# Two deferred tiles turned behind the first part of the next product

## The chip, the cores and the metric

The kernel runs on one core of a Trainium2 chip. The metric is the device time of one execution in microseconds; the median of the runs counts.

## The reference, cut to what matters

The program computes two blocks of two layers each on 512 tokens of width 1024. The first block mixes an mLSTM, a Fourier mix and a convolution, each layer followed by an MLP. The second block, where the change acts, projects the normed tokens by a wide matrix `w_in_2` and feeds a retention, a sparse attention with an index (`dsa`) and a gated linear attention (`gla`). At the start of each of its layers stand the projections of the index:

```python
h = rms_norm(x, pre_norm[l]) * (1.0 + scale[:, None]) + shift[:, None]
p = split_proj(h @ w_in[l])
q_idx = rope(q_idx, pos, IDX_ROT, ROPE_THETA)                        # 4 heads of 64: tiles DIQ 0, DIQ 1
k_idx_f = rope(k_idx[:, :, None], pos, IDX_ROT, ROPE_THETA)[:, :, 0] # 64 wide, laid twice: tile DIK
```

`rope` is x * cos + (x with its halves exchanged and one negated) * sin. The vectors `shift`, `scale` and `gate` come from products of a conditioning vector with `ada_w`, which the kernel spreads over its run.

## The kernel before, in words

**One list of steps for all engines.** `Order` writes a list of steps, and each of the five engine programs walks through it and emits its own share of a step (`mm` a part of a product, `ev` its evacuation from PSUM, `post` a piece of work after the evacuation, `split` the preparation of weights). The order of the list is so the order of each engine's instructions; a step that an engine has no share in doesn't touch its queue. Between engines there are semaphores. There is no second queue: an instruction that waits holds up all behind it on its engine.

**Products.** A float32 product of a weight tile (128 columns, 8 slices of 128 rows) and 512 tokens is 24 matmuls of 128x512: for each slice k, weight high half by token high half, weight low by token high, weight high by token low (L1012 to L1014). The weights come from HBM in slabs through a ring of six slots by SP (L920); ACT makes the high half (`split`, L2162, into WHI, two buffers), POOL the low half (L2572, in place in the ring as RGR). The split of unit u waits for the last matmul of unit u - 2. `place` puts the `split` steps into the list by an estimate of the time, in which `post` and `ev` cost nothing.

**Parts.** `task` cuts a product of 512 tokens into three parts: slices 0 to 2 (nine matmuls), 3 to 5 (nine), 6 and 7 (six). `run` puts the parts into the list. Behind each part comes what is woven in from beside (`weave`) and, behind the first, the turning of a modulation tile made by `filling` (`early`, list `soon`). Behind the last part it puts the `post` steps of the tiles that were left in `after`, and then the product's own `ev`. A tile whose evacuation is followed by more TensorE work (`roped`, `few`, `vheads`, the last tiles of a norm's output, `gateY`) is put into `after` by `task`, so each is worked on behind the next product, when its evacuation is over.

**abreast.** The first two products behind a norm are made side by side, slice by slice, since their tokens' slices come one by one (L356 to L379). Here `after` takes several: at the start of a layer of the second block the tiles DIQ 0 and DIQ 1, and with them the modulation tile (`ada`) that `self.laid` holds ready.

**The post of a rotated tile.** ACT evacuates the product into a buffer RAWS (L2322). TensorE multiplies it by a 128x128 permutation into bank PB7 (L1176, plain float32, two records), after DVE has read what PB7 held before. DVE multiplies the raw tile by the cosines (L1529), waits for TensorE, multiplies PB7 by the sines (L1532) and adds (L1534).

**The post of a modulation tile.** ACT copies the product's rows to WT (L2228), TensorE turns them by four small matmuls (L1142, L1143) into the bank of the tile, DVE adds the bias and writes MOD (L1515). The bank is free for the next product only then.

**The place.** In each of the two layers: DIQ 0 and DIQ 1 abreast (banks 1 and 0), `ada` (bank 1), DIK (bank 0), `post` DIQ 0, `post` DIQ 1, `post` ada, then `few` (20 columns wide, bank 1), `post` DIK, `post` few (transposes at L1185), and the product RQ 0.

Of the kernel before, what the change touches and what calls it, by code (L numbers as in the profile page):

```python
# [143 lines left out]
class Order:  # L144
# [54 lines left out]
    def run(self, n, parts, us):  # L199

        for part in parts:
            self.step("mm", n, part)
            self.early()
            self.weave(us / len(parts))
        for m in self.after:
            self.step("post", m)
        self.after = []
        self.step("ev", n)
        self.filling(us)
# [2511 lines left out]
```

## Time and profile before

| | |
|---|---|
| median of 3 runs | 3375.01 us (3374.52 to 3376.37) |
| the profiled execution | 3374.18 us |
| its span | 3372.4 us |
| mean granted TensorE clock | 0.939 |
| TensorE (PE) busy | 3063.9 us, 91% |
| DVE, ACT, POOL busy | 1419.1, 1010.1, 1044.4 us |
| PE idle before L1176, in all | 7.7 us behind DVE's L1534, four records |

How to read it: PE is the matmul side of TensorE, PEld its weight loads, DVE, ACT and POOL are VectorE, ScalarE and GpSimd, SP issues the loads. Times in the timelines are us from the start of the span. "idle before <-releaser" is the time that the engine stood still before the instruction, and the instruction that ended it. The granted clock is 1.00 at 2.4 GHz and 0.50 at 1.2 GHz.

### The profile page before, as it was taken

The numbers are of one execution on the slowest core, as the hardware profiler recorded it, in microseconds if no ns is written. First come the engines' busy times: TensorE is split into PE (matmuls) and PEld (weight loads), VectorE is DVE, ScalarE is ACT, GpSimd is POOL, SyncE is SP. The second block draws the span as 40 slices with busy tenths as digits, with TensorE's granted clock in tenths as the row PEclk, the third lists the DMA queues.
The fourth block names the chain that finished last, engine by engine and source line by source line (L and its number), as shares of the span: only waits on it lengthen the run. The fifth ranks groups of instructions, "written<-read, shape, count | busy, mean of one in ns | idle before, by whom it ended". The sixth has DMA issues, their size and how long they took to land.

```text
span 3372.4 us, 41180 instructions
## 1 busy us (share of the span) xinstructions
PE 3063.9 (91%) x16748; PEld 2460.5 (73%) x16748; DVE 1419.1 (42%) x2601; ACT 1010.1 (30%) x1640; POOL 1044.4 (31%) x508
## 2 busy tenths in 40 slices
PE   6899779899999979968999989999889989998898
PEld 4688568788888857757777776776668766775686
DVE  4583442513324356243521134734472346444722
ACT  3213432312213231342332332233423322334232
POOL 1121114122222312114344433232336422322455
PEclk9999878999999889978999989999999899999999
DMA  5332341111111123411322221121112221111122
GB/s 200 122 111 102 124 155 57 58 63 64 63 64 63 50 82 119 144 63 63 104 94 94 93 77 63 63 69 63 56 44 88 70 75 64 68 63 57 51 75 69
DMA packets 77707, 275.37 MB, mean 82 GB/s; under 512 B 8512, under 2 KB 10304, under 8 KB 77392
## 3 DMA queue, kind: packets, MB, share of 16 engines
q1 hardware_dynamic: 75824, 268.91, 23.7%
q10 hardware_dynamic: 1696, 3.84, 0.3%
q8 instruction: 133, 2.18, 0.3%
q14 instruction: 54, 0.44, 0.0%
HBM read 270.62 MB, written 2.10 MB: 81 GB/s over the span
## 4 chain that ended last, share of the span: by engine, by line
PE 78%; DVE 12%; ACT 4%; issue 3%; POOL 1%; DMA 1%; SPq 0%; DVEq 0%; ACTq 0%; POOLq 0%
PE pb L1012 19%; PE pb L1014 18%; PE pb L1013 18%; PE pb L1122 2%; PE pb L1034 2%; PE pb L1036 2%; PE pb L1035 2%; PE pb L961 2%; PE pb L1052 1%; PE pb L1054 1%; PE pb L1053 1%; DMA RG<-in_W_dram 1%; PE pb L1080 1%; DVE AR L1674 1%; POOL RGR L2572 1%
## 5 line engine op out<-in xcount | busy, mean ns | idle before, releaser
L2572 POOL TENSOR_TENSOR RGR<-RG,WHI 128x1024 fp32r<-128x1024 f32 x354 | 862.5, 2437 | 1896.1 <-ACT WHI L2162 1896.1
L2162 ACT ACTIVATE WHI<-RG 128x1024 fp32r<-128x1024 f32 x354 | 370.7, 1047 | 414.1 <-PE pb L1014 288.6
L1012 PE MATMUL pb<-HI,WHI 128*128 128x512 f32 (+1 forms) x880 | 379.0, 431 | 21.6 <-DVE MOD L1515 6.5
L1013 PE MATMUL pb<-HI,RGR 128*128 128x512 f32 (+1 forms) x880 | 355.2, 404 | 0.0
L1014 PE MATMUL pb<-LO,WHI 128*128 128x512 f32 (+1 forms) x880 | 355.2, 404 | 0.0
L1012 PE MATMUL pb<-HR,WHI 128*128 128x512 f32 (+1 forms) x768 | 278.8, 363 | 16.7 <-POOL RGR L2572 10.1
L1014 PE MATMUL pb<-HR,WHI 128*128 128x512 f32 (+1 forms) x768 | 277.8, 362 | 0.0
L1013 PE MATMUL pb<-HR,RGR 128*128 128x512 f32 (+1 forms) x768 | 277.5, 361 | 0.0
L1012 PE MATMUL pb<-HIDR,WHI 128*128 128x512 f32 (+1 forms) x768 | 273.7, 356 | 1.1 <-ACT RLT L2308 0.8
L1014 PE MATMUL pb<-HIDR,WHI 128*128 128x512 f32 (+1 forms) x768 | 274.7, 358 | 0.0
L1013 PE MATMUL pb<-HIDR,RGR 128*128 128x512 f32 (+1 forms) x768 | 274.2, 357 | 0.0
L1012 PEld LDWEIGHTS pb<-HI,WHI 128*128 128x128 f32 (+1 forms) x880 | 169.3, 192 | 92.5 <-issue 42.1
L1707 DVE TENSOR_TENSOR RLT<-RLT 128x256 f32<-128x256 f32 (+1 forms) x96 | 117.3, 1222 | 206.7 <-ACT RLT L2308 206.4
L1014 PEld LDWEIGHTS pb<-LO,WHI 128*128 128x128 f32 (+1 forms) x880 | 168.5, 191 | 44.7 <-issue 1.6
L1012 PE MATMUL pb<-HH,WHI 128*128 128x512 f32 (+1 forms) x464 | 173.9, 375 | 29.7 <-POOL RGR L2572 18.9
L1013 PEld LDWEIGHTS pb<-HI,RGR 128*128 128x128 f32 (+1 forms) x880 | 169.3, 192 | 38.9 <-issue 5.4
L1012 PEld LDWEIGHTS pb<-HR,WHI 128*128 128x128 f32 x768 | 146.9, 191 | 47.3 <-issue 24.3
L1013 PE MATMUL pb<-HH,RGR 128*128 128x512 f32 (+1 forms) x464 | 166.8, 359 | 0.0
L1014 PE MATMUL pb<-HL,WHI 128*128 128x512 f32 (+1 forms) x464 | 166.6, 359 | 0.0
L1014 PEld LDWEIGHTS pb<-HR,WHI 128*128 128x128 f32 x768 | 147.0, 191 | 22.9
L1012 PEld LDWEIGHTS pb<-HIDR,WHI 128*128 128x128 f32 x768 | 144.2, 188 | 26.5 <-issue 2.3
L1013 PEld LDWEIGHTS pb<-HR,RGR 128*128 128x128 f32 x768 | 147.1, 192 | 22.5
(407 smaller groups left out, 5637.4 us busy)
## 6 DMA issues: line engine op xcount, KB each, us to landing
RG<-in_W_dram SPq DMA_DIRECT2D x504, 512.0 KB, 3.5
XCX<-in_xT_dram ACTq DMA_DIRECT2D x4, 512.0 KB, 12.1
out_dram<-XCX SPq DMA_DIRECT2D x8, 256.0 KB, 2.1
CS<-in_CST_dram ACTq DMA_DIRECT2D x1, 1027.0 KB, 4.8
XCC<-in_ctxT_dram SPq DMA_DIRECT2D x4, 256.0 KB, 13.9
CS<-in_CST_dram SPq DMA_DIRECT2D x1, 523.0 KB, 4.7
RG<-in_W_dram SPq DMA_DIRECT2D x2, 256.0 KB, 2.7
RG<-in_W_dram SPq DMA_DIRECT2D x2, 128.0 KB, 3.5
```

The source lines that it names most:

```text
L961: i = e.matmul(PB[p["banks"][0]][32 * g:32 * g + 32, 0:256], CV[:, :, 4 * h + g], wt[:, g, :], start=h == 0, stop=h == 1, tile_position=(0 ...
L1012: e.matmul(out, hi[:, k, :], xh, start=k == order[0], stop=False)
L1013: e.matmul(out, lo[:, k, :], xh, start=False, stop=False)
L1014: i = e.matmul(out, hi[:, k, :], xl, start=False, stop=k == order[7])
L1034: e.matmul(out, xh[:, sl], hi[:, k, :], start=h == 0 and i0 % per == 0 and k == 0, stop=False)
L1035: e.matmul(out, xh[:, sl], lo[:, k, :], start=False, stop=False)
L1036: i = e.matmul(out, xl[:, sl], hi[:, k, :], start=False, stop=p["final"] and ends and k == nk - 1)
L1052: e.matmul(out, hi[:, k, :], xh, start=k == 0, stop=False)
L1122: m = e.matmul(sum_at(tag, c), squares_at(tag, i)[:, a:a + 128], ones[:, 0:1], start=k == 0 and c == first, stop=k == 7 and c == 5)
L1707: e.tensor_tensor(r, r, r, MUL).then_inc(*up("evacV", ("hidden", i)))
L2162: e.activation(WHI[:, u % 2, 0:n], RG[:, s % RING, 0:n], ACT.Copy).then_inc(*up("weightsA", u))
L2572: e.tensor_tensor(RGR[:, s % RING, 0:n], RG[:, s % RING, 0:n], WHI[:, u % 2, 0:n].bitcast(F32), SUB).then_inc(*up("weightsG", u))
```

## The change

`run` gets two lines. Behind the first part of a product (and behind each further one, where something is still left) it now puts the `post` steps of all tiles in `after` but the last. The last keeps its place behind the whole product.

```diff
@@ -201,6 +201,8 @@
         for part in parts:
             self.step("mm", n, part)
             self.early()
+            while len(self.after) > 1:
+                self.step("post", self.after.pop(0))
             self.weave(us / len(parts))
         for m in self.after:
             self.step("post", m)
```

## Rows read from the trace of the kernel before

**Rows 1.** The page: busy times, the chain by engine, the weight loads

```profile
PE 3063.9 (91%) x16748; PEld 2460.5 (73%) x16748; DVE 1419.1 (42%) x2601; ACT 1010.1 (30%) x1640; POOL 1044.4 (31%) x508
...
PE 78%; DVE 12%; ACT 4%; issue 3%; POOL 1%; DMA 1%; SPq 0%; DVEq 0%; ACTq 0%; POOLq 0%
...
RG<-in_W_dram SPq DMA_DIRECT2D x504, 512.0 KB, 3.5
```

**Rows 2.** Waits of TensorE, whole span: us in total, times, longest

```profile
PE pb L1012 <- DVE MOD L1515: 7.0, 4, 3.3
...
PE pb L1176 <- DVE AR L1534: 3.0, 2, 1.5
PE pb L1185 <- DVE AR L1534: 3.0, 2, 1.5
```

**Rows 3.** Timeline of the first place: start, us, engine, line, idle before

```profile
2019.95 0.47 PE L1012 MATMUL pb<-HI,WHI 128*128 128x512 f32 x1 [2.15 <-POOL RGR L2572]
...
2022.54 0.63 PE L1014 MATMUL pb<-LO,WHI 128*128 128x512 f32 x1
...
2022.96 0.63 PE L1012 MATMUL pb<-HI,WHI 128*128 128x512 f32 x1
...
2027.16 1.02 PE L1176 MATMUL pb<-AR,CS 128*128 128x512 f32 x2
2028.22 0.69 DVE L1532 TENSOR_TENSOR AR<-pb,TAB 128x512 f32<-128x512 f32 x1 [10.61 <-PE pb L1176]
2028.94 0.69 DVE L1534 TENSOR_TENSOR AR<-AR 128x512 f32<-128x512 f32 x1
...
2029.69 1.13 PE L1176 MATMUL pb<-AR,CS 128*128 128x512 f32 x2 [1.51 <-DVE AR L1534]
...
2030.65 0.28 PE L1142 MATMUL pb<-CS,WT 128*128 128x1 f32 x2
...
2030.79 0.36 PE L1143 MATMUL pb<-CS,WT 128*128 128x1 f32 x2
...
2031.41 2.34 POOL L2572 TENSOR_TENSOR RGR<-RG,WHI 128x1024 fp32r<-128x1024 f32 x1 [11.12 <-ACT WHI L2162]
2031.58 2.72 DVE L1534 TENSOR_TENSOR AR<-AR 128x512 f32<-128x512 f32 x1
2034.22 0.15 DVE L1515 TENSOR_TENSOR MOD<-pb,VC 128x2 f32<-128x2 f32 x1
...
2034.42 0.62 PE L1012 MATMUL pb<-HI,WHI 128*20 128x512 f32 x1 [3.27 <-DVE MOD L1515]
...
2038.22 0.40 PE L1012 MATMUL pb<-HI,WHI 128*20 128x512 f32 x1
...
2041.69 1.02 PE L1176 MATMUL pb<-AR,CS 128*128 128x512 f32 x2
```

**Rows 4.** Windows: stretch, length, PE PEld DVE ACT POOL busy, PEclk, DMA, GB/s

```profile
2021.00:2024.20 3.20, 3.20 (x9) 2.48 (x8) 0.00 (x0) 0.00 (x0) 0.00 (x0) 0.51 0.63 248
...
2034.50:2037.90 3.40, 3.40 (x9) 1.22 (x10) 0.47 (x1) 0.00 (x0) 0.00 (x0) 0.50 0.00 0
...
2042.80:2044.20 1.40, 0.00 (x0) 0.00 (x0) 1.33 (x2) 0.62 (x1) 0.64 (x1) 1.00 0.93 295
2044.90:2048.20 3.30, 3.30 (x9) 2.59 (x8) 0.00 (x0) 0.00 (x0) 1.49 (x1) 0.51 0.00 0
```

**Rows 5.** Timeline of the second place

```profile
2719.30 1.12 PE L1176 MATMUL pb<-AR,CS 128*128 128x512 f32 x2 [1.51 <-DVE AR L1534]
...
2724.03 0.62 PE L1012 MATMUL pb<-HI,WHI 128*20 128x512 f32 x1 [3.27 <-DVE MOD L1515]
```

**Rows 6.** Timeline around the first place: ada's turning, ACT, POOL, DVE

```profile
2016.27 0.28 PE L1142 MATMUL pb<-CS,WT 128*128 128x1 f32 x2
...
2016.80 0.16 DVE L1515 TENSOR_TENSOR MOD<-pb,VC 128x2 f32<-128x2 f32 x1 [4.44 <-PE pb L1143]
2016.91 0.69 DVE L1529 TENSOR_TENSOR AR<-AR,TAB 128x512 f32<-128x512 f32 x1
2017.21 0.59 ACT L2322 ACTIVATE AR<-pb 128x512 f32<-128x512 f32 x1
2017.45 2.84 POOL L2572 TENSOR_TENSOR RGR<-RG,WHI 128x1024 fp32r<-128x1024 f32 x2 [28.18 <-ACT WHI L2162]
...
2042.75 0.69 DVE L1532 TENSOR_TENSOR AR<-pb,TAB 128x512 f32<-128x512 f32 x1 [7.78 <-PE pb L1176]
```

## The prediction

> **What bounds the kernel.** The page comes first: TensorE is busy for 91% of the span, and 78% of the chain that ended last lies on it [rows 1]. A change therefore counts by what it does to the time in which TensorE stands still and to the clock at which it runs. Next, TensorE's waits [rows 2]. They are many and short. Three kinds lie where this change acts: 1.5 us before the rotation at L1176, 1.5 us before the transposes at L1185 (both twice), and up to 3.3 us before a product's first matmul at L1012, behind a DVE addition at L1515. Third, the order of the steps: `after` holds more than one entry at the start of `run` at only two places of the program, the first ordinary product (DIK) of each layer of the second block. There it holds three, the rotations of DIQ 0 and DIQ 1 and the turning of a modulation tile (ada), all left by `abreast`. Everywhere else, the norms' sums among them, at most one waits and the new loop doesn't turn. The timeline of the first place [rows 3] and windows over it [rows 4] carry the sum; [rows 5] show that the second repeats it to some hundredths of a us.
>
> **The place before** [rows 3]. DIK starts at 2019.95. Its 24 matmuls end where rotation 0 starts, at 2027.16: 7.21 us. Rotation 0 takes 1.02 us; then TensorE waits 1.51 us while DVE multiplies (0.69) and adds (0.69). Rotation 1 starts at 2029.69, the ada turning at 2030.65, and its small matmuls end at 2031.15. The next product (few) takes the bank in which the ada result sits. DVE empties that bank only behind rotation 1, and the addition L1534 there takes 2.72 us instead of 0.69, as it meets POOL's weight split (2031.41, 2.34 us). So L1515 runs at 2034.22 and few at 2034.42, after 3.27 us idle. Its 24 matmuls last until 2041.69, 7.27 us. From DIK's start to few's end: 21.74 us.
>
> **What the change does to each queue.** DVE, ACT, POOL and SP have no step between DIK's parts here, so their instructions keep their order. Only TensorE's changes: two rotations (four matmul records) move ahead of DIK's last 15 matmuls, the ada turning stays behind DIK, nothing is added. Queued behind the moved waits is the rest of DIK, so the 1.51 us for rotation 0 are still paid, now inside it. What goes is the wait for DVE's work on rotation 1, which gets the 15 matmuls as cover. The inputs are there in time: ACT has copied both by 2017.80, DVE has done its first multiplication by 2017.60 [rows 6].
>
> **The sum for the first place.**
> - DIK's first nine matmuls: 2019.95 to 2022.96 as before, 3.01 us.
> - Rotation 0 starts at 2022.96, with a granted clock of 0.5 (1.2 GHz) until 2024.2 or so [rows 4]. No row here shows a rotation begun at that clock. Its bounds are 1.02 us and twice that; the matmuls beside it take 0.42 us from start to start instead of 0.23, so I take 1.75. With 1.44 for DVE and 0.05 to resume it is 3.24, and rotation 1 starts at 2026.20. DVE meets no split here: POOL is through at 2020.29 and its next one needs ACT, behind DIK [rows 3, 6].
> - Rotation 1: about 0.86 to the next issue.
> - DIK's last 15 matmuls. The prices are those of few: nine in 3.80 us, 0.422 each, at the low clock, then 15 in 3.47, 0.231 each, at 2.4 GHz [rows 3, 4]. Does the clock hold? After the idle time before few, and after the 1.5 us behind few, the granted clock was 0.5 from 2034.5 to 2037.9 and from 2044.9 to 2048.2 [rows 4]. The moved stall is as long, so I take it that eight matmuls run slow here: 3.38 + 1.62 = 5.00 us. Bounds: none slow 3.5, all slow 6.3.
> - From DIK's end to few: the held ada tile was turned and added without a queue in front, from 2016.27 to 2016.96 [rows 6]; with 0.05 to resume 0.75 us, where there were 0.50 and 3.27. DVE's work on rotation 1 is done by 2028.6; a whole POOL split on top, 2.34, would still be covered.
> - few: 4.8 us of idle in two stalls stood before it and nine of its matmuls were slow. Now some 0.25 us stands there, and the low stretch is spent in DIK: 24 x 0.231 = 5.54. Bounds 5.5 and 7.3.
>
> Together 3.01 + 3.24 + 0.86 + 5.00 + 0.75 + 5.54 = 18.40 us against 21.74: **3.34 us less**. 3.0 of it is idle time; the rest is the clock.
>
> What is late next: DIK ends at 2032.1 instead of 2027.2. POOL's split for the product after few moves with it, from 2031.41 to about 2033.8, ends by 2036.2 and is wanted at 2041.2; 5 us of cover, beyond which each us would cost one. SP's load into DIK's slot goes out 4.9 us later and serves the fifth product after few, at least five times 5.5 us away; it lands in 3.5 us [rows 1].
>
> **Does it last?** DVE stood idle for 10.6 us before this place and for 7.8 us behind few [rows 3, 6], so no backlog reaches across, and the loads follow the matmuls. All that comes after moves up as a whole, and the second place saves as much: 6.7 us. The profiled execution took 3374.18 us, its span 3372.4; the median of the runs, 3375.01, is 0.83 above it. 3374.18 - 6.7 = 3367.5 for such an execution, **3368.3 us** for the median, 0.20% less. A measurement of this kernel tells about 0.2%, 6.75 us, from no change.
>
> **Rivals.**
> *The clock holds* inside DIK. Its rest then takes 3.5 us: 4.8 per place, 9.7 in all, 3365.3; if the fall behind few goes as well, 1.6 more per place, 3362. For it: the idle has matmuls close on both sides. Against it: a stall of that length (2042.8 to 2044.2) was followed by the low clock [rows 4]. The Trainium skill, on the page "TensorE: Matmul & The Clock Gate", section on HAM oscillation, puts the return to half rate down to long waits between groups of matmuls; by that rule this rival would be the outcome, and this trace, with its 1.5 us, disagrees.
> *Given back.* The idle goes, yet few runs nine matmuls slow beside DIK's eight. Then 3.34 - 9 x 0.19 = 1.6 per place: 3371.8. For it: each stall had a low stretch of its own. Against it: only 0.25 us is left before few.
> *Slower.* The stop inside DIK lets the clock fall and keeps it down through DIK's rest and few. Then 3.0 + 3.2 + 1.7 + 6.3 + 1.0 + 10.1 and 0.9 for the next rotation make 26.2 us, 4.5 lost per place: 3384. It decides from 24 slow matmuls behind rotation 0 on (the nine of before, and the 3.0 us of idle over 0.19 each). Against it: both times the clock came back after eight or nine matmuls without a break.
> *It doesn't do what it says*, as nowhere else do two entries wait. That is taken in above; if the two places didn't bring their 3.0 us either, the time would stay at 3375.
>
> **How the numbers follow.** Forecast 0.50, clock holds 0.28, given back or next to nothing 0.17, slower 0.05. The forecast's own spread, 3366.5 to 3370, lies across the bound of 0.2% at 3368.3, half on each side. Faster: 0.28 + 0.25 = 0.53. Same: 0.25 + 0.17 = 0.42. Slower: 0.05. The range runs from 3362.5 (both gains of the clock) to 3372.0 (given back).
>
> **What would show it.** Right: L1176 starts near 2023.0 and 2026.2, behind nine matmuls of DIK; no addition L1534 here takes over 0.7 us; few waits some 0.25 us, starts near 2032.8 and runs at the high clock; the granted clock is 0.5 in DIK's rest; the same about 686 us later; the span is near 3365.7. Wrong: over 1 us of wait before few, a low clock in few, a DVE operation of over 2 us at this place, or a new wait for POOL at the product behind few.

## The result, and the profile after

The changed kernel took **3358.3 us** (median of 4 runs, 3354.24 to 3359.23), the kernel before, run beside it, 3374.77 (4 runs, 3372.47 to 3376.37). The ratio is **0.9949**, its 95% interval 0.9932 to 0.9967: 16.5 us less, where 6.7 were forecast, and below the range that was given. Two further comparisons on other chips gave 0.9968 (0.9956 to 0.9979) and 0.9971 (0.9960 to 0.9983). The changed kernel is faster each time, by 0.3 to 0.5%. Its profiled run took 3354.24 us, its span 3352.1. Line numbers below are those of the kernel before plus 2.

The page after, its line of busy times, which answers to the first of [rows 1]:

```profile
PE 3055.5 (91%) x16748; PEld 2453.9 (73%) x16748; DVE 1416.1 (42%) x2601; ACT 1010.4 (30%) x1640; POOL 1044.4 (31%) x508
```

The same instructions. TensorE is busy for 8.4 us less (3063.9 to 3055.5) with the same 16748 matmuls, so a good part of the gain is matmuls that took less time, at a higher granted clock as the windows below show; DVE's 3.0 us less are about what it saves at the two places (7.80 to 5.96 us in each, by the windows further down), where it no longer meets POOL.

TensorE's waits, whole span (us in total, times, longest); they answer to [rows 2]:

```profile
PE pb L1178 <- DVE AR L1536: 3.0, 2, 1.5
PE pb L1187 <- DVE AR L1536: 3.0, 2, 1.5
PE pb L1014 <- DVE MOD L1517: 1.0, 4, 0.3
```

The two waits of 3.27 us are 0.25 now; the other two kinds stand as before. That is the 3.0 us per place of the forecast.

Timeline of the first place after; it answers to [rows 3]:

```profile
2019.95 0.47 PE L1014 MATMUL pb<-HI,WHI 128*128 128x512 f32 x1 [2.15 <-POOL RGR L2574]
...
2023.01 1.75 PE L1178 MATMUL pb<-AR,CS 128*128 128x512 f32 x2
...
2026.26 1.12 PE L1178 MATMUL pb<-AR,CS 128*128 128x512 f32 x2 [1.51 <-DVE AR L1536]
2026.82 0.80 PE L1014 MATMUL pb<-HI,WHI 128*128 128x512 f32 x1
...
2028.15 0.69 DVE L1536 TENSOR_TENSOR AR<-AR 128x512 f32<-128x512 f32 x1
...
2030.72 0.28 PE L1144 MATMUL pb<-CS,WT 128*128 128x1 f32 x2
...
2031.47 0.41 PE L1014 MATMUL pb<-HI,WHI 128*20 128x512 f32 x1 [0.25 <-DVE MOD L1517]
...
2032.61 2.40 POOL L2574 TENSOR_TENSOR RGR<-RG,WHI 128x1024 fp32r<-128x1024 f32 x1 [12.32 <-ACT WHI L2164]
...
2037.03 1.02 PE L1178 MATMUL pb<-AR,CS 128*128 128x512 f32 x2
```

The order is the one foreseen. POOL's split now starts at 2032.61, behind DVE's work on both rotations; the addition takes 0.69 us, where it took 2.72. The clock is another matter (windows of the changed kernel, columns as in [rows 4]):

```profile
2023.00:2026.20 3.20, 1.75 (x3) 0.33 (x1) 1.38 (x3) 0.00 (x0) 0.00 (x0) 0.77 0.04 14
2026.40:2030.60 4.20, 4.20 (x17) 3.08 (x18) 1.79 (x3) 0.00 (x0) 0.00 (x0) 1.00 0.02 4
...
2039.20:2042.50 3.30, 2.95 (x15) 2.47 (x16) 0.30 (x1) 0.18 (x1) 2.54 (x1) 1.00 0.18 71
```

The first stretch holds the stall inside DIK, the second the rest of DIK, at 1.00 where 0.5 was forecast. The third follows the 1.51 us stall behind few; before, the granted clock was 0.5 there [rows 4].

To compare whole traces I cut the program at four matmuls: a **place** runs from DIK's first matmul to the matmul 88 later, in RQ 1; a **remainder** from there to the next place or the last matmul. The windows of place 1, remainder 1, place 2, remainder 2, before:

```profile
2019.95:2052.63 32.68, 26.39 (x88) 16.28 (x89) 7.80 (x10) 3.65 (x6) 5.50 (x3) 0.79 0.19 66
2052.63:2709.55 656.92, 604.84 (x3187) 470.33 (x3186) 308.21 (x558) 208.91 (x327) 248.38 (x118) 0.96 0.21 66
2709.55:2742.17 32.62, 26.33 (x89) 16.17 (x89) 7.80 (x10) 3.65 (x6) 5.50 (x3) 0.79 0.18 66
2742.17:3359.02 616.85, 572.73 (x3030) 443.33 (x3029) 284.93 (x525) 193.04 (x302) 237.36 (x111) 0.98 0.19 63
```

and after:

```profile
2019.95:2046.42 26.47, 23.20 (x88) 14.24 (x89) 5.96 (x10) 3.65 (x6) 5.59 (x3) 0.94 0.23 79
2046.42:2699.29 652.87, 602.56 (x3188) 467.74 (x3186) 308.18 (x558) 208.92 (x327) 248.48 (x118) 0.96 0.21 67
2699.29:2725.75 26.46, 23.19 (x88) 14.34 (x89) 5.96 (x10) 3.65 (x6) 5.58 (x3) 0.94 0.23 78
2725.75:3338.65 612.90, 570.61 (x3031) 440.76 (x3029) 284.90 (x525) 193.06 (x302) 237.47 (x111) 0.98 0.19 63
```

Each place is 6.2 us shorter, not 3.3. And each remainder, in which the change moves no instruction, is 4.0 us shorter: 2.3 and 2.1 us of that are less time busy, 1.8 in each are less time standing still. 2 x 6.2 + 2 x 4.0 = 20.4 us; the rest of the program took as long in these two profiled runs (both reach the place at 2019.95), whose times are 3374.18 - 3354.24 = 19.9 us apart.

A window's mean clock gives the time at 1.2 GHz in it: (1 - PEclk) x 2 x length. Before, a place had 0.42 x 32.68 = 13.7 us at 1.2 GHz, the 3.27 us of idle before few among them, so 10.5 us of matmuls. After it has 0.12 x 26.47 = 3.2 us. Three stretches of matmuls ran at half rate before (at DIK's start, in few, behind few [rows 4]); one such stretch is left. The matmul time saved in a place, 26.39 - 23.20 = 3.2 us, is what this difference in the clock gave back.

### The profile page after: what moved, and what is told of

Its sections match the earlier page's. It is cut to its first block, busy times and chain, and to the rows that moved or that the text cites. A ratio compares the mean times of both kernels' runs of the same rounds, so it can differ in the third digit from the quotient of the medians.

```text
span 3352.1 us, 41180 instructions
## 1 busy us (share of the span) xinstructions
PE 3055.5 (91%) x16748; PEld 2453.9 (73%) x16748; DVE 1416.1 (42%) x2601; ACT 1010.4 (30%) x1640; POOL 1044.4 (31%) x508
## 4 chain that ended last, share of the span: by engine, by line
PE 78%; DVE 12%; ACT 4%; issue 3%; POOL 1%; DMA 1%; SPq 0%; DVEq 0%; ACTq 0%; POOLq 0%
PE pb L1014 19%; PE pb L1016 18%; PE pb L1015 18%; PE pb L1124 2%; PE pb L1036 2%; PE pb L963 2%; PE pb L1038 2%; PE pb L1037 2%; DMA RG<-in_W_dram 1%; PE pb L1054 1%; POOL RGR L2574 1%; PE pb L1056 1%; PE pb L1055 1%; PE pb L1082 1%; DVE AR L2085 1%
## 6 DMA issues: line engine op xcount, KB each, us to landing
XCC<-in_ctxT_dram SPq DMA_DIRECT2D x4, 256.0 KB, 13.9
```

## The experiments

Three theories were to be told apart. **Idle and clock**: the removed wait gives its own 3.0 us, and the low stretches behind it go too. **Collision**: what mattered was DVE's addition beside POOL's split. **Alignment**: the remainders turn on how TensorE stands to the changes of its clock when it comes out of a place. Beside every group of kernels the kernel before ran on the same chip: 3373.55 us (30 runs) beside the first four, 3375.51 (15) beside e5 to e8, 3370.61 (16) beside e9 to e11. The lengths here are of the profiled run of each, read as above; the medians are of all runs. The expectations cut at other matmuls: their places are about 2 us shorter than those of the table (24.5 for 26.47), their remainders about 1 and 2 us longer (657.9 for 656.92, 619.0 for 616.85).

| kernel | median us | ratio (95%) | place 1 | remainder 1 | place 2 | remainder 2 |
|---|---|---|---|---|---|---|
| before | 3374.77 | | 32.68 | 656.92 | 32.62 | 616.85 |
| e8_before | 3376.82 (1 run) | | 32.67 | 656.93 | 32.64 | 616.79 |
| after | 3358.30 | 0.9949 | 26.47 | 652.87 | 26.46 | 612.90 |
| e1_again | 3361.47 | 0.9968 (0.9956-0.9979) | 26.43 | 656.96 | 26.45 | 612.81 |
| e10_change | 3362.27 | 0.9971 (0.9960-0.9983) | 26.45 | 656.89 | 26.48 | 612.83 |
| e2_fill | 3372.37 | 0.9994 (0.9986-1.0003) | 29.52 | 657.05 | 29.52 | 619.93 |
| e3_pool_later | 3364.81 | 0.9973 (0.9964-0.9981) | 25.86 | 654.18 | 31.51 | 614.46 |
| e4_layer0 | 3371.67 | 0.9996 (0.9988-1.0005) | 26.40 | 656.90 | 32.66 | 616.92 |
| e5_shift | 3372.66 | 0.9992 (0.9983-1.0001) | 33.35 | 652.82 | 33.32 | 612.85 |
| e6_spread | 3363.27 | 0.9964 (0.9950-0.9977) | 25.93 | 656.81 | 25.92 | 616.79 |
| e7_spread_few | 3357.56 | 0.9947 (0.9935-0.9960) | 22.77 | 659.22 | 21.16 | 615.44 |
| e9_ada_first | 3366.65 | 0.9988 (0.9979-0.9997) | 26.09 | 659.89 | 26.10 | 616.77 |
| e11_spread_few | 3357.17 | 0.9959 (0.9947-0.9972) | 21.17 | 655.37 | 22.80 | 619.80 |

**e1_again: the change once more.** No edit.

> The changed kernel once more, to see how far its time and its places of low clock are the same from run to run. Two theories for the 10 us beyond the forecast. Clock theory: with the stall before few gone, TensorE's granted clock stays at 1.0 in few and in the product behind it, at both places, in every run: 16 us less, ratio 0.9950 to 0.9956, and the two places take 24.5 us each from DIK's start as in the first trace. Chance theory: which stretches get the low clock is luck, the place's true gain is 3.3 us each and the first runs were lucky: ratio nearer 0.998, and the low stretch shows up inside DIK's rest or behind few in this trace.

3361.47 us. Its trace repeats both places to 0.04 us and remainder 2 to 0.1, while remainder 1 has the length of before. The third trace of the change, e10_change, was taken beside e9 and e11:

> The changed kernel, beside the spread version on one chip. Places of 24.5 and 24.3 us, the second layer's end in its short form, 615.0; the first layer's remainder 653.8 or 657.9 by where the first 2020 us leave the clock. Median 11 to 16 us below the kernel before.

3362.27 us, with the same four lengths as e1. So 6.2 us per place and 4.0 in remainder 2 repeat; the 4.0 in remainder 1 came in one of three traces. By the four lengths e1 and e10 are 16.4 us below the kernel before, by medians 12.1 and 8.3, which is less than e10's expectation (11 to 16). In the traces a part of such a difference lies in front: the same code up to the first place took between 2019.06 and 2027.90 us, so the times of two traced runs carry some us of that, and the cut lengths don't. Whether it explains the medians too, no run shows: they hold runs without a trace, and of the kernel before only two runs were cut up.

In e1 the low stretch of place 1 isn't at DIK's start (window 2023.14:2026.40) but behind few (2042.80:2046.10). Windows of e1_again, columns as before:

```profile
2023.14:2026.40 3.26, 3.19 (x11) 1.96 (x11) 0.03 (x1) 0.00 (x0) 0.34 (x1) 1.00 0.76 292
2029.60:2033.80 4.20, 3.95 (x21) 2.91 (x20) 1.52 (x4) 1.30 (x2) 0.00 (x0) 1.00 0.06 17
2042.80:2046.10 3.30, 3.30 (x10) 2.60 (x10) 0.00 (x0) 0.00 (x0) 0.55 (x1) 0.61 0.00 0
```

Its place 2 has it at DIK's start again. The length of the place is the same either way, but the remainder behind it isn't. The change was traced in seven places, two in each of its three traces and one in that of e4_layer0 below. In four the low stretch lay at DIK's start, and the remainder behind was the short one; in three it lay behind few (place 1 of e1, of e10 and of e4), and the remainder was the long one. For e10, at DIK's start and behind few:

```profile
2020.30:2026.00 5.70, 4.19 (x14) 2.48 (x15) 1.99 (x3) 0.00 (x0) 0.29 (x1) 1.00 0.47 184
2039.10:2042.50 3.40, 3.40 (x10) 2.63 (x9) 0.00 (x0) 0.00 (x0) 1.35 (x1) 0.50 0.00 0
```

So in these seven places the clock at DIK's start already told which remainder would follow. That is an order seen in the traces; no run set it on purpose.

**e2_fill: the waits stay, TensorE works in them.** Five throwaway matmuls behind rotation 0, twelve behind the ada turning, into a bank that is free there; nothing uses their result.

```diff
-        for m in self.after:
+        queued = len(self.after)
+        for i, m in enumerate(self.after):
             self.step("post", m)
+            if queued == 3 and i == 0:
+                self.step("spin", 5, 3)
+        if queued == 3:
+            self.step("spin", 12, 3)
...
+        def spin(count, bank):
+            for _ in range(count):
+                e.matmul(PB[bank][:, :], HI2[:, 0, 0:128], HI2[:, 1, :], start=True, stop=True)
```

> The kernel before, with throwaway matmuls (5 and 12 of 128x512 into a free bank, 1.2 and 2.8 us) put into the two stalls of each place. The waits stay as they are, TensorE is only busy in them. Clock theory: few's nine slow matmuls become fast (1.75 us per place) and the product behind few too, perhaps; with what follows in the layer 3 to 5 us per place, so 3367 or less, ratio 0.996 to 0.998. Idle theory (only the time in which TensorE stands still counts): no gain, ratio 1.000. Chance theory: ratio between 0.999 and 1.001.

Timeline and window of e2_fill, place 1:

```profile
2030.62 1.12 PE L1181 MATMUL pb<-AR,CS 128*128 128x512 f32 x2 [0.36 <-DVE AR L1543]
...
2031.94 2.97 PE L1487 MATMUL pb<-HI 128*128 128x512 f32 x12
2035.42 0.41 PE L1017 MATMUL pb<-HI,WHI 128*20 128x512 f32 x1 [0.51 <-DVE MOD L1524]
```
```profile
2022.41:2051.93 29.52, 27.14 (x105) 17.67 (x106) 7.87 (x10) 3.64 (x6) 5.57 (x3) 0.94 0.20 73
```

The waits for DVE are all still there, and only 0.36 and 0.51 us of the two stalls are left unfilled. The work added brings nothing, and yet the place is 3.16 us shorter: its mean clock is 0.94 in place of 0.79, with the same 3 us or so at 1.2 GHz as under the change. That is the clock's share of the 6.2 us by itself: with the two stalls filled, two of the three slow stretches are gone. In the sum half of the 2 x 3.1 us was lost, since remainder 2 came out 3.1 us longer, and the median shows nothing (0.9994), where 0.996 to 0.998 was expected.

**e3_pool_later: the collision alone.** The kernel before, but POOL's split of RQ 0's weights waits until DVE has done with rotation 1.

```diff
+        held_back = {}
+        for m, p in enumerate(o.pieces):
+            if p["how"] == "few":
+                held_back[p["unit"] + 1] = m - 3
...
+            if u in held_back:
+                e.wait_ge(*at("evacV", ("roped", held_back[u])))
```

> The kernel before, but at the two places POOL's weight split for the product behind few waits until DVE's addition for rotation 1 is through. If the 2.72 us addition is DVE held up by POOL, it takes 0.69 us, few starts 2.03 us earlier and waits 1.24 instead of 3.27 us: 4.1 us less in all, ratio 0.9988, and more only if the clock changes with it. If the addition is long for another reason, it stays at 2.7 us and the ratio at 1.000 or above. The clock theory adds: two stalls of 1.5 and 1.2 us are still there, so few still starts at the low clock.

Timeline and windows (places 1 and 2) of e3_pool_later:

```profile
2037.99 0.69 DVE L1534 TENSOR_TENSOR AR<-AR 128x512 f32<-128x512 f32 x1
...
2038.81 0.41 PE L1012 MATMUL pb<-HI,WHI 128*20 128x512 f32 x1 [1.24 <-DVE MOD L1515]
...
2038.85 2.75 POOL L2579 TENSOR_TENSOR RGR<-RG,WHI 128x1024 fp32r<-128x1024 f32 x1 [10.62 <-DVE MOD L1515]
```
```profile
2027.90:2053.76 25.86, 21.60 (x89) 13.49 (x89) 5.77 (x10) 3.64 (x6) 5.92 (x3) 1.00 0.23 79
2707.94:2739.45 31.51, 27.25 (x89) 16.44 (x90) 5.77 (x10) 3.64 (x6) 5.90 (x3) 0.78 0.18 66
```

The addition takes 0.69 us, few waits 1.24 instead of 3.27. So 2.03 of the 3.27 us were the collision, and with the split out of the way 8.7 us of the program went (0.9973) with no matmul moved, more than the 2 x 2.03 us of idle time and the 0.9988 expected from them. The two places have the same instructions, the same idle time (4.26 us) and lengths 5.65 us apart: one had the full clock throughout, the other 0.44 x 31.51 = 13.9 us at 1.2 GHz. This is what the clock alone can do to such a place. It also limits what e2 says: in place 1 here the two stalls ahead of few (1.51 and 1.24 us) cost no low stretch at all.

**e4_layer0: half the change.** The new loop in the first of the two layers only.

```diff
+            while len(self.after) > 1 and self.pieces[n]["l"] == 0:
+                self.step("post", self.after.pop(0))
```

> The change in the first layer of the second block alone. Clock theory and idle theory both: half of the whole gain. If the gain is made in each layer by itself, 8 us less, ratio 0.9976, with 6.2 us of it at the place and the rest in the remainder of that layer. If the second layer gains only because the first shifts its phase against the clock's, the second place here is not as before, and the ratio is away from 0.9976 by more than 0.001.

Place 1 has the new length (26.40), place 2 the old one (32.66), and remainder 2, whose code and place are those of before, has the old length to 0.07 us. The expected ratio, 0.9976, wasn't reached: remainder 1 took its long form. The median moved by 1.9 us only, with an interval that holds no change, where the four lengths give 6.2. The profiled run reached the first place 3.6 us later than that of before; whether the other runs did so too, no trace tells.

**e5_shift: added work.** The kernel before, with three throwaway matmuls ahead of RQ 1 in each layer; the waits of the place are untouched.

```diff
+        if self.pieces[n]["how"] == "roped" and self.pieces[n]["dst"] == "RQ" and self.pieces[n]["jj"] == 1:
+            self.step("spin", 3, 3)
```

> The kernel before, with three throwaway matmuls (0.7 us) in front of the product RQ 1 in each layer of the second block, behind the place, and nothing else. Phase theory: the remainder of a layer has a long and a short form (657.9 or 653.8 us in the first layer, 619.0 or 615.0 in the second, the same to 0.1 us in all traces so far), and which it takes hangs on how TensorE stands to the clock's changes when it leaves the place. The 0.7 us put the second layer into the short form: its end takes 615.7 us with the added work instead of 619.0, and the first layer 654.5 or stays at 658.6. So 2.5 to 6.6 us less in spite of added work. Theory of work alone: 1.4 us more, both remainders 0.7 longer, no low stretch fewer.

Windows of e5_shift: remainder 1, remainder 2:

```profile
2054.56:2707.38 652.82, 602.57 (x3188) 468.32 (x3186) 307.47 (x558) 208.29 (x327) 248.40 (x118) 0.96 0.21 67
...
2740.70:3353.55 612.85, 570.63 (x3030) 441.32 (x3029) 284.22 (x525) 192.43 (x302) 237.39 (x111) 0.98 0.20 63
```

Each place is 0.7 us longer, as the three matmuls cost, and each remainder 4.0 us shorter, to 0.05 us the two remainders of `after`. So a remainder can be short with every wait of the place left standing and no engine relieved. That the 0.7 us are the cause is likely for remainder 2, which was long in both traces of the kernel before; it rests on this one trace, and it doesn't tell coming later from TensorE being busier just ahead. It isn't steady: the eleven runs lie between 3367.55 and 3379.95 us, and the median (0.9992) can't be told from no change.

**e6_spread: all three pieces spread over DIK.** The ada turning and rotation 0 behind its first part, rotation 1 behind its second.

```diff
-        for part in parts:
+        if len(self.after) == 3:
+            early, self.after = [self.after[2:] + self.after[:1], self.after[1:2], []], []
+        else:
+            early = [[]] * len(parts)
+        for i, part in enumerate(parts):
...
+            for m in early[i]:
+                self.step("post", m)
```

> From the kernel before: behind DIK's first part the ada turning and rotation 0, behind its second part rotation 1, nothing behind the whole. The 1.5 us stall inside DIK goes, since the second part covers DVE's work on rotation 0, and the 0.25 us before few. Both theories: 1.7 us of idle less per place than in the changed kernel, so a place of 22.8 us instead of 24.5 and 30.7, about 3.5 us below the changed kernel, ratio 0.995 to 0.996. Clock theory: no low stretch within the place but the one at DIK's start or the one behind few. If the stall was needed for nothing but DVE, this is the better version.

Place 1 of e6_spread:

```profile
2024.35:2050.28 25.93, 24.42 (x89) 15.79 (x89) 6.60 (x11) 3.65 (x6) 5.57 (x3) 0.87 0.23 81
```

TensorE stands still for 25.93 - 24.42 = 1.51 us, where 3.27 are left under the change: 1.76 us less idle. Yet the place is only 0.54 us shorter, because 0.26 x 25.93 = 6.7 us of it are at 1.2 GHz instead of 3.2, and remainder 2 is the long one (616.79). 3363.27 us, 12.2 below the kernel before, where the change gave 16.5, 12.1 and 8.3: no better than the change, and short of its expected ratio.

**e7_spread_few and e11_spread_few: no wait left.** e6, and few's transposes go behind the first part of RQ 0.

```diff
+        if tasks[-1]["how"] == "few":
+            self.soon, self.after = self.soon + self.after, []
+            return
```

> As the run before, and the transposes of few go behind the first part of RQ 0, so the 1.5 us stall behind few goes too. Place of 21.3 us, another 1.5 us less idle per place, and the low stretch behind few can't start: 1.6 us more where it was there. 3358 us or less, ratio 0.9945 to 0.9955. If the remainder of a layer falls into its long form by the new phase, 4 us per layer are given back, to 3363.

> The spread version with the transposes of few behind RQ 0's first part, again, for a comparison with the change on one chip. Places of 19 to 21 us against 24.4: 9 us less by the places, of which the remainders give back 2 to 8, since they took 660.2 and 617.6 us in its first trace. 2 to 6 us below the changed kernel; if the remainders take their short form, 9.

The two places of e7_spread_few:

```profile
2025.08:2047.85 22.77, 22.77 (x88) 14.63 (x89) 6.60 (x11) 3.65 (x6) 5.60 (x3) 0.93 0.27 92
2707.07:2728.23 21.16, 21.16 (x88) 13.49 (x89) 6.60 (x11) 3.65 (x6) 5.60 (x3) 1.00 0.26 91
```

TensorE is busy from end to end. 3357.56 us on one chip, 3357.17 on another, where the change took 3362.27: 5.1 us less again, the fastest on that chip. The single runs of the two overlap (3356.40 to 3362.22 against 3358.75 to 3364.50). With 3.7 to 5.3 us less in each place than the change it might have brought more; its remainders are 655.4 and 659.2, 615.4 and 619.8 us long, longer than the short forms of the change by 2.5 to 6.9.

**e8_before: the kernel before, a second trace.** No edit.

> The kernel before, unchanged, for a second trace. Phase theory: both places 30.5 to 30.8 us with 10.5 us at the low clock, the second layer's end 619.0 us; only the first 2020 us of the program and the first layer's remainder (657.9 or 653.8) may differ from the first trace. Chance theory: the places and the second layer's end differ between the two traces as well.

All four lengths repeat those of before to 0.06 us. That is no rule for the other kernels: remainder 1 of the change took both of its lengths, and e7 and e11, the same kernel, differ by up to 4.4 us in a stretch.

**e9_ada_first: another order, all behind DIK.** The ada turning goes ahead of the two rotations; no matmul moves into DIK.

```diff
+        if len(self.after) == 3:
+            self.after = self.after[2:] + self.after[:2]
```

> From the kernel before: both rotations stay behind DIK, only the order of the three queued steps is changed, the ada turning first, then rotations 0 and 1. Bank theory: few waited not for the rotations but for the ada addition queued behind them on DVE; with ada first few starts right behind rotation 1, the 3.27 us are gone without any cover by DIK, and idle time per place is 3.0 us (two stalls of 1.5), as in the changed kernel or 0.25 below it. Cover theory (the prediction's words): the 15 matmuls of DIK are what hides DVE's work; then a wait of some 2 to 3 us before few or behind it stays. Bank theory gives a place of 24 to 26 us, by how the clock falls, and 8 to 16 us less in all.

Timeline and window of e9_ada_first, place 1:

```profile
2029.24 1.13 PE L1178 MATMUL pb<-AR,CS 128*128 128x512 f32 x2 [1.51 <-DVE AR L1536]
...
2030.97 2.40 POOL L2574 TENSOR_TENSOR RGR<-RG,WHI 128x1024 fp32r<-128x1024 f32 x1 [11.57 <-ACT WHI L2164]
2031.13 2.79 DVE L1536 TENSOR_TENSOR AR<-AR 128x512 f32<-128x512 f32 x1
```
```profile
2019.06:2045.15 26.09, 23.07 (x89) 14.55 (x89) 8.61 (x11) 3.65 (x6) 5.58 (x3) 0.93 0.21 81
```

The collision is there in full, 2.79 us, and nobody waits for it: few's bank is empty before. The idle time of the place is 26.09 - 23.07 = 3.02 us, 0.25 less than under the change, and the place 0.4 us shorter. So the 3.27 us were an order on DVE (the small addition that frees few's bank, queued behind the rotation), and moving matmuls into DIK was one way of several to be rid of them. The remainders are long here (659.89 and 616.77), and the median is 4.0 us below before (0.9988) where 8 to 16 were expected, and 4.4 above the change on the same chip.

## Why the prediction was wrong, step by step

**Right: the places and the queues.** Two places, TensorE's order alone, DVE without a collision, no new wait behind it. The idle time went as forecast, 3.27 to 0.25 us, and the 1.51 us for rotation 0 stayed, inside DIK. Rotation 0 at the low clock took 1.75 us, the value taken between 1.02 and twice that.

**The sum of the first place**, term by term against the timeline after: 3.06 for 3.01; 3.25 for 3.24; 0.56 for 0.86; **3.90 for 5.00**; 0.75 for 0.75; 5.56 for 5.54. Together 17.08 us instead of 18.40.

**The step that failed first: "I take it that eight matmuls run slow here."** None did: the granted clock is 1.00. Rotation 1 and this term take 4.46 us together, where 0.86 and the lower bound of 3.5 make 4.36. The inference was from stretches behind two stalls to a third, a stall of the same length. The windows it rested on [rows 4] leave one out, that of the 3.27 us wait itself (kernel before):

```profile
2031.20:2034.40 3.20, 0.00 (x0) 0.00 (x0) 3.17 (x4) 0.07 (x1) 2.34 (x1) 0.52 0.00 0
```

The clock was low there almost from the wait's first moment, 2031.15. So it hadn't fallen because of that wait, and the low stretch in few went on from it. Nor does the length of the wait show in it: place 2 of e3, with 1.24 us for 3.27, has as much time at 1.2 GHz. The same step was wrong in its other half, that the stretch behind few stays slow: the sum ended at few, which counts that stretch as it was before. From few's end to the cut it took 32.68 - 21.74 = 10.94 us and takes 26.47 - 17.08 = 9.39 now, 1.55 less. 3.34 + 1.32 + 1.55 = 6.21 us, the measured difference. In the places themselves the rival "the clock holds", in its second form (3362 us), is what happened, 6.2 for its 6.4 per place; it had been given 0.28 with the first form. Where a measured gain comes near the 6.7 us of the forecast, as the 8.3 of e10 does, that is luck: its places are 6.2 and 6.1 us shorter as well.

What decides isn't the length of the stall alone. In all six places of the three traces of the change, the stall of 1.51 us inside DIK left the clock at 1.00; the equal one behind few left it at 1.00 in four and was followed by 0.5 in two, the two in which DIK's start had run at the full clock. In e6 both places ran slow at DIK's start and behind few as well, so that isn't a rule either. Of the kernel before e2 shows that the two stalls ahead of few, 1.51 and 3.27 us, went with two low stretches: with both filled, one is left. The rule of the Trainium skill that the prediction weighed (page "TensorE: Matmul & The Clock Gate", section on HAM oscillation: half rate comes back after long waits between groups of matmuls) agrees with the stall inside DIK. The stretch behind few in e1 speaks against it, as [rows 4] did.

**The step that failed second: "All that comes after moves up as a whole."** It rested on waits and loads alone. But the clock doesn't move up with the code, and with the clock the waits change too. Two of TensorE's kinds of wait that lie in the remainders, whole span, before and then after:

```profile
PE pb L1436 <- DVE AR L2069: 19.2, 10, 2.7
PE pb L1052 <- ACT AR L2368: 6.1, 2, 3.1
```
```profile
PE pb L1438 <- DVE AR L2071: 14.4, 8, 2.4
PE pb L1054 <- ACT AR L2370: 4.1, 2, 2.0
```

e5 has the sums of after, e4 and e8 those of before, and e1 and e10, with one long and one short remainder, 16.8 and 5.1. Windows of three of five parts of remainder 2, cut at the same matmuls, before:

```profile
2742.17:2797.91 55.74, 53.91 (x302) 43.70 (x301) 30.29 (x70) 13.80 (x20) 20.91 (x8) 0.97 0.23 76
2797.91:3059.93 262.02, 246.16 (x1302) 184.19 (x1300) 133.28 (x297) 84.13 (x153) 80.19 (x36) 0.99 0.20 65
...
3102.99:3165.99 63.00, 49.66 (x302) 39.48 (x300) 45.12 (x47) 21.13 (x25) 27.78 (x13) 0.89 0.16 51
```

after:

```profile
2725.75:2779.96 54.21, 52.38 (x301) 42.50 (x300) 30.29 (x70) 13.80 (x20) 20.93 (x8) 1.00 0.24 78
2779.96:3043.56 263.60, 247.99 (x1301) 185.68 (x1299) 133.41 (x297) 84.13 (x153) 80.94 (x36) 0.98 0.20 64
...
3086.64:3145.54 58.90, 47.16 (x301) 36.56 (x300) 44.88 (x47) 21.14 (x25) 27.80 (x13) 0.94 0.17 54
```

The first part is 1.5 us shorter after, the second 1.6 longer, so that this is given back; then comes a part of 63.0 us that now takes 58.9, at 0.94 instead of 0.89, and the difference stays to the end (the parts not shown are equal to 0.1 us). Of its 4.1 us, 2.5 are less time busy and 1.6 less standing still, and both waits named above lie in it. The first of these forks can be seen at one wait. Behind the same 1.83 us on DVE, the clock falls in one kernel and holds in the other (window of before, then of after, at the same matmuls):

```profile
2792.60:2795.90 3.30, 3.30 (x8) 2.63 (x9) 0.00 (x0) 0.07 (x1) 2.38 (x1) 0.50 0.02 9
```
```profile
2776.10:2779.40 3.30, 3.27 (x14) 2.68 (x15) 0.00 (x0) 0.15 (x1) 2.40 (x1) 1.00 0.02 6
```

Eight matmuls in one, fourteen in the other. At the same matmuls e5 has fourteen too, and with them the remainder lengths of `after`, though its place has the waits of before. So this fork doesn't need what the change does to the place. That it is chosen by the moment at which TensorE arrives fits all traces and is argued, not shown.

So by the four lengths the change takes 16.4 or 20.4 us: 6.0 of idle time and 6.4 of clock in the two places, and 4.0 or 8.0 in stretches with the same instructions, where the granted clock differs and some waits with it. The mechanism of the forecast was half right; its term for the clock and the claim that nothing else moves were not. What stays open: what makes the clock fall or hold at a given stall. Neither the stall's length nor the kernel settles it, and no run tried arrival times in small steps. Nor do the runs tell what ahead of place 1 decides where its low stretch falls, or why the medians on two chips show less than the four lengths.

## What to carry to other kernels

When a short stall is taken off TensorE, ask for the matmuls behind it too: here 3.0 us of idle time held another 3.2 of half-rate matmuls, and filling the stall with throwaway matmuls (e2) measures that share without touching a wait. Compare traces stretch by stretch, cut at the same matmul; a gain or loss in a stretch that the edit doesn't touch can come with the granted clock alone, can be as large as the edit's own, and doesn't tell whether the edit is good. And before moving work to cover a wait, look at what is queued in front of the small operation that ends it: one reordering (e9) removed as much idle time, though the run as a whole gained less by it than by the change.

## What the runs showed of the hardware that was not expected

- In the one trace with three throwaway matmuls (0.7 us) ahead, each of two stretches of over 600 us, with the same instructions, was 4.0 us shorter than before (656.92 to 652.82, 616.85 to 612.85).
- Two places with the same instructions and the same 4.26 us of idle time took 25.86 and 31.51 us in one execution (e3), at a mean clock of 1.00 and 0.78.
- One stall of 1.51 us between full stretches of matmuls was followed by a granted clock of 0.61 over 3.3 us in one execution and 1.00 in another of the same kernel (behind few, e1 and `after`).
- The clock was low (0.52) from the start of a wait of 3.27 us on, so it had not fallen because of that wait (kernel before).
- The lengths that one stretch takes repeat to 0.15 us from trace to trace: remainder 2 took 612.90, 612.81, 612.83 and 612.85 us in four, 616.85, 616.79, 616.92, 616.79 and 616.77 in five, and lengths between or above in the other four (614.46, 615.44, 619.80, 619.93).
